# Leaving out the keep-warm matmuls in the heads of the norms and of the third output stage

## The reference

```
h = rms_norm(x, ln_mix_pre);  proj = h @ w_in            # sb, dil
x = x + rms_norm(o @ w_out, ln_mix_post)                 # out2
h = rms_norm(x, ln_ffn_pre);  g, u = split(h @ w_gate_up)  # ffn_up
x = x + rms_norm((silu(g) * u) @ w_down, ln_ffn_post)    # ffn_down
gate = sigmoid(rms_norm(x, ln_pli) @ w_pli_gate)         # gate
x = x + gate * (p @ w_pli_proj)
```

## Time and profile before

| | |
|---|---|
| time, median of 3 | 3027.54 us (3026.38 to 3034.44) |
| time of the profiled execution | 3030.63 us |
| its span, first to last instruction | 3028.8 us |
| mean granted clock of TensorE | 0.994 |
| TensorE busy | 2950.3 us, 97% |
| VectorE busy | 1828.4 us, 60% |
| ScalarE busy | 1367.8 us, 45% |
| read from memory | 511.55 MB, 170 GB/s |
| records of line 1655 | 264 (52 into aux, 212 into main) |

### The profile page before, as it was taken

The page is one execution under the profiler, slowest core; times in us unless marked ns, Lnnn a source line. Parts: engine busy times, 40 slices in busy tenths (PEclk is TensorE's granted clock), DMA queues, the critical chain, the costliest instruction groups (busy, mean ns, idle before and its releaser), DMA issues.

```text
span 3028.8 us, 41594 instructions
## 1 busy us (share of the span) xinstructions
PE 2950.3 (97%) x14729; PEld 2477.7 (82%) x14729; DVE 1828.4 (60%) x2315; ACT 1367.8 (45%) x1890; POOL 111.3 (4%) x114
## 2 busy tenths in 40 slices
PE   7999999999999999999999999999999999999999
PEld 4678887788887889988888899997788888878877
DVE  6878878788774345544445677665545445444454
ACT  6732222433343244434444577674544444434353
POOL 0000000000110000001110000000000000000000
PEclk9999999999999999999999999999999999999999
DMA  8855545444554225543334555555555555555545
GB/s 279 305 186 188 184 173 191 153 161 151 199 183 163 93 100 187 186 134 109 106 108 145 168 156 155 158 160 171 158 186 182 185 182 183 185 195 188 188 154 167
DMA packets 144277, 515.12 MB, mean 170 GB/s; under 512 B 16240, under 2 KB 16288, under 8 KB 142256
## 3 DMA queue, kind: packets, MB, share of 16 engines
q1 hardware_dynamic: 141264, 495.01, 49.2%
q0 software_dynamic: 2912, 18.74, 1.7%
HBM read 511.55 MB, written 2.13 MB: 170 GB/s over the span
## 4 chain that ended last, share of the span: by engine, by line
PE 57%; ACT 2%; DVE 2%; issue 2%; DMA 0%; ACTq 0%; DVEq 0%; SPq 0%
PE main L1582 47%; PE main L1575 6%; PE aux L1535 1%; ACT w_hi L580 1%; PE aux L1717 0%; PE aux L1708 0%; DVE w_lo L983 0%; PE aux L1555 0%; DVE h_lo L1105 0%; DMA raw<-in_w_sb 0%; ACT L804 0%; PE aux L1768 0%; ACT h_hi L690 0%; PE main L1655 0%; DVE u L1267 0%
## 5 line engine op out<-in xcount | busy, mean ns | idle before, releaser
L983 DVE TENSOR_TENSOR w_lo<-raw,w_hi 128x1024 fp32r<-128x1024 f32 x836 | 1039.1, 1246 | 876.2 <-ACT w_hi L580 865.7
L580 ACT ACTIVATE w_hi<-raw 128x1024 fp32r<-128x1024 f32 x836 | 880.1, 1058 | 1297.0 <-PE main L1582 973.8
L1582 PE MATMUL main<-w_hi,h_hi 128*128 128x512 f32 (+1 forms) x1472 | 561.9, 382 | 6.4 <-DVE h_lo L1232 3.1
L1582 PE MATMUL main<-w_lo,h_hi 128*128 128x512 f32 (+1 forms) x1472 | 552.4, 375 | 0.0
L1582 PE MATMUL main<-w_hi,h_lo 128*128 128x512 f32 (+1 forms) x1472 | 552.4, 375 | 0.0
L1582 PE MATMUL main<-w_hi,act_hi 128*128 128x512 f32 (+1 forms) x1408 | 536.4, 381 | 10.6 <-ACT u L720 6.5
L1582 PE MATMUL main<-w_hi,act_lo 128*128 128x512 f32 (+1 forms) x1408 | 528.2, 375 | 0.0
L1582 PE MATMUL main<-w_lo,act_hi 128*128 128x512 f32 (+1 forms) x1408 | 527.7, 375 | 0.0
L1575 PE MATMUL main<-act_hi,w_hi 128*128 128x256 f32 (+1 forms) x960 | 321.7, 335 | 3.7 <-DVE act_lo L1087 2.8
L1575 PE MATMUL main<-act_hi,w_lo 128*128 128x256 f32 (+1 forms) x960 | 320.5, 334 | 0.0
L1575 PE MATMUL main<-act_lo,w_hi 128*128 128x256 f32 (+1 forms) x960 | 320.4, 334 | 0.0
(11 more groups left out here) (269 smaller groups left out, 2491.2 us busy)
## 6 DMA issues: line engine op xcount, KB each, us to landing
raw<-in_w_ffn_up SPq DMA_DIRECT2D x176, 512.0 KB, 3.3
gates<-in_w_side SPq DMA_DIRECT2D x128, 512.0 KB, 3.4
raw<-in_w_in_ret SPq DMA_DIRECT2D x128, 512.0 KB, 4.0
raw<-in_w_in_conv SPq DMA_DIRECT2D x120, 512.0 KB, 4.1
raw<-in_w_out SPq DMA_DIRECT2D x96, 512.0 KB, 3.3
raw<-in_w_ffn_down SPq DMA_DIRECT2D x88, 512.0 KB, 4.2
raw<-in_w_mod SPq DMA_DIRECT2D x64, 512.0 KB, 4.7
raw<-in_w_sb SPq DMA_DIRECT2D x64, 384.0 KB, 3.1
```

The source lines that it names most:

```text
L580: A(w_hi[:, slot, :], raw[:, slot, :], ACT.Copy).then_inc(hi_split, 1)
L983: V.tensor_tensor(out=w_lo[:, slot, :], in0=raw[:, slot, :], in1=w_hi[:, slot, :].bitcast(F32), op=ALU.subtract).then_inc(lo_split, 1)
L1582: ins = mm(bank[:, c0:c1], x, w_part[:, slot, j * n + c0:j * n + c1], start=(k == 0 and j == 0 and i == 0), stop=(k == (7 if name == "gate ...
```

## The change

All calls of `stay_warm` go, and the function too: 132 matmuls, 8 + 26 in layer 1's head, 26 + 10 in sb's, 14 in out2's, 18 + 6 in ffn_up's and in gate's. All waits stay where they are, so the instruction that follows a removed group now carries the wait that stood ahead of it. No other instruction is added, removed or moved, on any engine.

```
-            def stay_warm(bank, n):
-                for _ in range(n):
-                    mm(bank[:, 0:P], mat("ident"), mat("ones"), start=True, stop=True)
...
-            def norm_head(n, T, xs, before, warm):
+            def norm_head(n, T, xs, before):
                 def step(k):
                     for kg in norm_groups(k):
                         if kg == 0:
                             if T == 2:
                                 pe.wait_ge(free_a, done_a[before] - (1 if before in ("ffn_up", "gate") else 0))
                                 pe.wait_ge(free_d, done_d[before] - 1)
-                            stay_warm(main[0] if T == 2 else aux[3], warm[0])
                         norm_T(n, T, xs, kg)
                     if k == 0:
                         if T == 4:
                             pe.wait_ge(free_d, done_d[before])
-                        stay_warm(main[0], warm[1])
                     if k % 2 == 0:
                         pe.wait_ge(s["h_ready"], 4 * prep_index(n) + k // 2 + 1)
...
-norm_head(1, 4, xs4, "in1_conv", (26, 8))      +norm_head(1, 4, xs4, "in1_conv")
-norm_head(3, 2, None, "sb", (26, 10))          +norm_head(3, 2, None, "sb")
-norm_head(5, 2, None, "ffn_up", (18, 6))       +norm_head(5, 2, None, "ffn_up")
-norm_head(7, 2, None, "gate", (18, 6))         +norm_head(7, 2, None, "gate")
...
             def out2_split(j):
                 if j == 0:
                     pe.wait_ge(free_a, done_a["out2"] - 1)
                     pe.wait_ge(free_d, done_d["out2"] - 1)
-                    stay_warm(main[0], 14)
```

More of the change, by code:

```diff
@@ L1851, in _ @@
                 channels = lambda par: [(conv_bank(L, par, i)[0], sec * P, W, conv_bank(L, par, i)[1]) for i, sec in enumerate((2, 1, 3, 0))]
-                phase(f"in{L}_conv", nothing if L == 0 else norm_head(1, 4, xs4, "in1_conv", (26, 8)), lambda e, par, k: None, channels)
+                phase(f"in{L}_conv", nothing if L == 0 else norm_head(1, 4, xs4, "in1_conv"), lambda e, par, k: None, channels)
                 def ret_start(k):
@@ L1878, in _ @@
             attn_parts = lambda par: rows(h_hi, h_lo, 2, [(t, main[2 * par + t], 0, 384) for t in range(2)])
-            sb_norm = norm_head(3, 2, None, "sb", (26, 10))
+            sb_norm = norm_head(3, 2, None, "sb")
             def sb_start(k):
@@ L1904, in out2_split @@
                     pe.wait_ge(free_d, done_d["out2"] - 1)
-                    stay_warm(main[0], 14)
             phase("out2", lambda k: last_head(front, back, out2_split, k), lambda e, par, k: None, two(h_hi, h_lo), ready=lambda k: pe.wait_ge(s["p_lo_ready"], 16 + k + 1))
-            phase("ffn_up", norm_head(5, 2, None, "ffn_up", (18, 6)), ffn_up, two(h_hi, h_lo))
+            phase("ffn_up", norm_head(5, 2, None, "ffn_up"), ffn_up, two(h_hi, h_lo))
             def down_ready(k):
@@ L1916, in _ @@
             phase("ffn_down", lambda k: ffn_up(21, 1, k), lambda e, par, k: None, two(f_hi, f_lo), ready=down_ready)
-            gate_norm = norm_head(7, 2, None, "gate", (18, 6))
+            gate_norm = norm_head(7, 2, None, "gate")
             def gate_start(k):
```

## The result

| | before | changed |
|---|---|---|
| time, median of 7 | 3029.77 us (3026.38 to 3035.68) | 3042.35 us (3034.71 to 3042.9) |
| ratio | | 1.0033, 95% interval 1.0023 to 1.0043 |
| span of the profiled execution | 3028.8 us | 3037.6 us |
| mean granted clock of TensorE | 0.994 | 0.988 |
| TensorE records | 14729 | 14465 (264 fewer) |

The changed kernel is slower by 0.33%, 10.0 us of 3029.77; the medians are 12.6 us apart. The forecast was 10 us more, 3037.5 us, in a range of 3030 to 3044. It started from 3027.54 us, the median of 3 runs; the median of the 7 is 2.2 us higher, so 3042.35 us lies 4.8 us above the forecast time while the ratio meets the forecast difference.

The account below looks back on a forecast made before the run. TensorE, busy 97% of the span, was taken to bound the kernel. Terms 1.7 + 1.4 + 0.7 + 3.0 + 3.0 = 9.8 us on the median 3027.54 gave 3037.3, written as 3037.5 us, range 3030 to 3044.

Parts of the forecast that it names:

- The keep-warm matmuls stand in gaps: All five heads: about 30 us of keep-warm on TensorE fills waits and is not on the path.
- Holes of 5 us and more drop the clock: Layer 1, sb, ffn_up, gate: holes of 5 us or more drop TensorE's clock nearly always; out2's 2.9 us often.
- First transposes: Norm heads: first transposes run at half clock, +1.7 us for layer 1's 16, +0.9 us for 8 elsewhere.
- Half clock on the pieces, 2.1 us: Heads of sb, ffn_up, gate: 4.6 us of weight pieces at half clock lose 2.1 us (1.3 to 2.8).
- Layer 1, +1.7: Layer 1's head: first transposes delay VectorE's chain 1.7 us throughout, TensorE's half-clock pieces covered; bounds 0 to +3.
- ffn_up and gate, +3.0 each: Both heads: transposes +0.9 us and half-clock pieces 2.1 us, nothing covered, +3.0 us each (1.8 to 3.8).
- out2, +0.7: out2: transposes start 0.3 us sooner, clock fall two chances in three, costing up to 1.5 us; +0.7 (-0.3 to +1.5).
- sb, +1.4: sb's head: about +1.9 us after 1.05 us covered, part perhaps lost in a 7.87 us DMA; +1.4 (0.4 to 2.5).
- rival (a): Layer 1 and sb: waits cover the delays, sb's perhaps wholly; about 5 us more in all, 3032 us; chance 0.12.
- rival (b): Four heads: clock returns more slowly, one more short stretch each, 6 us more, 3043.5 us; chance 0.07.
- Rule against row: out2's 2.9 us hole: skill page implies no fall, sum 8.9 us; forecast followed the trace row, fall after 2.04 us.
- Transposes: Layer 1: by the page's rule transposes don't count for the clock, pieces start at half clock, term nearer 2.5 than 1.7.

Follow-up runs that it names:

- the second groups alone: Against the kernel before, only keep-warm behind the second transposes kept (8, 10, 6, 6); first groups and out2's 14 left out: ratio 1.0008 (0.9999 to 1.0017).
- shorter first groups: Against the kernel before, keep-warm ahead of the first transposes cut to 17, 17, 7, 12, 12, second groups unchanged: ratio 1.0006 (0.9997 to 1.0015).
- those with the transposes: Against the kernel before, every keep-warm matmul replaced by two transposes of the same 128 columns: ratio 1.0003 (0.9993 to 1.0012).

## Why the prediction was right, point by point

- **The keep-warm matmuls stand in gaps.** Right. Taking 30 us of work off TensorE made no instruction of the path earlier but one: layer 1's first piece (start difference 3.64 before it, 1.64 at it), which its half-clock pieces then gave back (3.57 at the third transposes).
- **Holes of 5 us and more drop the clock.** Right in all four heads of three traces (two of the changed kernel, and that with the second groups alone; out2's hole apart) and in the two heads of the one with only ffn_up and gate out. out2's hole of 2.95 us had a fall in all three traces that have it; I had given it two chances in three.
- **First transposes.** +1.7 us for 16: measured 1.71 (1.93 to 3.64). +0.9 us for 8, up to the first piece: measured 1.05 in ffn_up (2.22 to 3.27) and 0.87 in gate (6.39 to 7.26). Of each, 0.2 us is a later start of the first transpose (2.22 to 2.43 us in ffn_up), which I did not have; the transposes themselves are 0.84 and 0.67 us slower. In gate the clock fell 0.2 us after the first of them had started.
- **Half clock on the pieces, 2.1 us (1.3 to 2.8).** Measured 1.54 in ffn_up and 1.53 in gate, about 3.4 us of work at half clock instead of my 4.6; in the kernel with only ffn_up and gate out, ffn_up lost 2.7 us (1.34 to 4.08), the other end of the range. I had taken the middle because I took the long stretch of before to have a second hole. It had none: from 1110.05 to its end at 1115.7 TensorE never stood. And in gate it is not one stretch that reaches into the pieces, as I had it, but a second fall behind the 2.10 us hole, in all three traces that have this hole (2.1 to 2.2 us).
- **Layer 1, +1.7.** Measured 1.64 and 1.60, but the number is right by luck, and the path is not the one described. I had VectorE's chain 1.7 us later throughout and TensorE's losses covered. In both traces, though, ScalarE waits for TensorE at the third transposes, before and then changed:

```profile
1123.92 1.93 ACT L669 ACTIVATE u<-aux,sideT,mod_a 128x256 f32<-128x256 f32 x4 [2.79 <-PE aux L1535]
```

```profile
1127.49 1.93 ACT L669 ACTIVATE u<-aux,sideT,mod_a 128x256 f32<-128x256 f32 x4 [2.72 <-PE aux L1535]
```

TensorE does not stand between the first piece and them, so its half-clock pieces are paid in full: the first piece is 0.29 us sooner against the stage's start, and 1.93 us are lost behind it. With the second groups alone the first transposes are 1.70 us late too, but the pieces run at full clock, and the head costs 1.08 us: VectorE's chain alone would not have cost 1.7.
- **ffn_up and gate, +3.0 each.** Measured 2.59 and 2.40, in the other traces up to 3.79; mechanism right but for gate's second fall, size a little high.
- **out2, +0.7.** Measured 1.34 and 1.54: the fall came each time and at most 0.2 us of its 1.5 was covered, and the transposes did not start 0.3 us sooner as I had it (start difference 2.42 before them, 2.41 at them).
- **sb, +1.4.** Mis-sized in both traces: 0.23 and 3.16 us. Up to the third transposes, where I had about +1.9, they lose 1.2 us (2.15 to 3.32) and 4.1 us (1.63 to 5.75), by the length of the half clock. Behind them both gain 0.9 us, since the wait for the raw weights that stands in before's chain is gone. That is not a delay that vanishes in a wait, as rival (a) had it: with shorter first groups TensorE reaches the third transposes with no delay (start difference -0.06), and gains 0.95 us all the same. The five traces with a fall in sb's head gain 0.5 to 0.95 us there; those with the transposes and with only ffn_up and gate out, without a fall, gain 0.1 us or nothing. Why is open. The term was a guess over something that varies by 3 us.
- **Sum.** 9.8 forecast, 8.2 in the heads of one trace and 11.4 in the other; 10.0 by the ratio of the times. That it meets the ratio within 0.2 us is luck: ffn_up and gate came out 1.0 us lower together, out2 0.6 us higher, and sb could have come out on either side. Two sums were off: the upper bounds add up to 4.8 us over the forecast, which is about 3042 us and not 3044, so the top of the range stands on rival (b) alone; and without a fall in out2 the sum is 9.1, or 8.8 with the 0.3 us, not 8.9.
- **Rule against row.** For out2 I followed the row (a fall after 2.04 us) against the Trainium skill, page "TensorE: Matmul & The Clock Gate", section "Why this matters for your kernels" (no gaps of more than about 3 us). The runs agree with the row: falls behind holes of 1.89, 2.21, 2.48 and 2.95 us. But holes of 1.89 to 2.75 us also stood without one.
- **Transposes.** The same page's section "Part 4: PE-mode transpose" has them not counting for the clock. For these fp32 transposes the measurement says otherwise: 36 of them in ffn_up's hole held it at 1.00, where an empty hole dropped it in all four traces that have it.

## What to carry to other kernels

Work that TensorE does in a wait cost nothing here as long as it ended before the wait did, and fp32 transposes did as well as fp32 matmuls; what it protects is the speed of the work behind the wait. Look at every hole of about 2 us and more beside a dense stage, also the ones behind the transposes: a small group close ahead of the real work may be worth as much as a large one at the hole's start. Set two traces against each other record by record, since falls of the clock at untouched places are as large as the effects sought.

## What was not expected of the hardware

The same hole may or may not drop the clock: 2.21 us without and with a fall in one and the same trace. Three holes are the same in the eight traces whose kernels add nothing to them: 1.89 us (ffn_down) had a fall in three of the eight, 2.04 us (2074.87 of before) in six, 2.6 to 2.75 us (1139.94 of before) in three. In this range the length alone does not tell. From layer 1 to gate, none of the ten traces has a fall behind a hole of 1.4 us or less, and every hole of 5 us or more has one. In ffn_up a 12-record group of keep-warm behind half-clock transposes saw the clock back 0.36 us ahead of the first piece. In sb, ffn_up and gate the first transpose behind an empty hole of 5 to 6 us started 0.2 us later against its operand than before; in layer 1, behind 7.08 us, it did not, nor in gate behind 2.21 us at half clock. The cause is open.
